# Prompt attention of a hybrid decoder step: probabilities turned unnormalised, product with V in query rows, one scaling per query tile, two score banks

## What is computed

```python
lo = jnp.einsum('bhqd,bhld->bhql', q, k_own) * HD_B ** -0.5
lo = jnp.where(own_pos[None, :] <= q_pos[:, None], lo, -jnp.inf)
p = jax.nn.softmax(concatenate([selected past block, lo]), axis=-1)
o = einsum(p, v)            # (512, 8, 64), all float32
```

## Time and profile before

| what | value |
|---|---|
| runs (3) | 1193.85, 1194.81, 1203.77 us; median 1194.81 |
| profiled execution | 1196.35 us, its span 1194.5 us |
| mean granted PE clock | 0.938 |
| busy | PE 1087.3 us (91%), DVE 648.0 (54%), ACT 468.7 (39%), POOL 256.4 (21%) |
| attention stage | 225.4 to 347.3 us of the span |

### The profile page before, as it was taken

The page is one execution under the profiler, slowest core; times in us unless marked ns, Lnnn a source line. Parts: engine busy times, 40 slices in busy tenths (PEclk is TensorE's granted clock), DMA queues, the critical chain, the costliest instruction groups (busy, mean ns, idle before and its releaser), DMA issues.

```text
span 1194.5 us, 21266 instructions
## 1 busy us (share of the span) xinstructions
PE 1087.3 (91%) x8054; PEld 1013.5 (85%) x8054; DVE 648.0 (54%) x892; ACT 468.7 (39%) x707; POOL 256.4 (21%) x113
## 2 busy tenths in 40 slices
PE   6999899698988589879968999999999999999997
PEld 6999799665677479668758799999999999999997
DVE  5228987897725774676544426555433433433443
ACT  6423554324333544554534122234413413523443
POOL 0035566776300353353330000000000000000000
PEclk8999899858998899989978899999999999999999
DMA  8376777655410245644547115433333332223311
GB/s 283 93 238 197 247 222 208 202 163 169 139 38 1 53 141 150 178 132 141 161 135 190 53 44 170 127 105 89 89 89 89 99 96 88 88 88 90 100 56 72
DMA packets 179256, 152.67 MB, mean 128 GB/s; under 512 B 8913, under 2 KB 141723, under 8 KB 178918
## 3 DMA queue, kind: packets, MB, share of 16 engines
q1 hardware_dynamic: 137414, 124.72, 35.5%
q10 hardware_dynamic: 41768, 26.91, 7.9%
HBM read 142.77 MB, written 8.93 MB: 127 GB/s over the span
## 4 chain that ended last, share of the span: by engine, by line
PE 76%; DVE 11%; ACT 5%; issue 4%; POOL 2%; ACTq 1%; DVEq 0%; POOLq 0%
PE ps L416 57%; PE ps L1795 6%; PE ps L1782 3%; DVE lg L1029 2%; POOL v_low L574 2%; PE ps L1682 1%; PE ps L1696 1%; DVE w_low L405 1%; PE ps L1539 1%; PE ps L1672 1%; ACTq L390 1%; DVE v_low L1261 1%; ACT v_high L827 1%; PE ps L1902 1%; ACT w_high L400 1%
## 5 line engine op out<-in xcount | busy, mean ns | idle before, releaser
L400 ACT ACTIVATE w_high<-w_raw 128x1024 fp32r<-128x1024 f32 x125 | 132.5, 1060 | 423.1 <-PE ps L416 399.8
L416 PE MATMUL ps<-xh,w_high 128*128 128x256 f32 x1216 | 257.5, 294 | 13.3 <-DVE w_low L405 7.4
L405 DVE TENSOR_TENSOR w_low<-w_raw,w_high 128x1024 fp32r<-128x1024 f32 x125 | 160.4, 1284 | 193.9 <-ACT w_high L400 193.6
L416 PE MATMUL ps<-xl,w_high 128*128 128x256 f32 x1216 | 250.0, 288 | 0.0
L416 PE MATMUL ps<-xh,w_low 128*128 128x256 f32 x1216 | 249.6, 287 | 0.0
L416 PEld LDWEIGHTS ps<-xh,w_high 128*128 128x128 f32 x1216 | 193.3, 194 | 21.1 <-issue 20.2
L416 PEld LDWEIGHTS ps<-xl,w_high 128*128 128x128 f32 x1216 | 193.7, 193 | 0.0
L416 PEld LDWEIGHTS ps<-xh,w_low 128*128 128x128 f32 x1216 | 193.6, 193 | 0.0
L557 POOL TENSOR_TENSOR ring<-ring,qb 128x1024 f32<-128x1024 f32 x64 | 158.5, 2488 | 158.7 <-DMA ring<-in_cache_k 87.0
L416 PE MATMUL ps<-mh,w_high 128*128 128x256 f32 (+1 forms) x640 | 129.3, 283 | 2.4 <-issue 2.4
L416 PE MATMUL ps<-mh,w_low 128*128 128x256 f32 (+1 forms) x640 | 129.5, 284 | 0.0
(11 more groups left out here) (358 smaller groups left out, 1498.0 us busy)
## 6 DMA issues: line engine op xcount, KB each, us to landing
ring<-in_cache_k SPq DMA_DIRECT2D x128, 256.0 KB, 3.0
ring<-in_cache_v SPq DMA_DIRECT2D x128, 256.0 KB, 2.9
w_raw<-in_w_in ACTq DMA_DIRECT2D x74, 256.0 KB, 4.0
w_raw<-in_w_up SPq DMA_DIRECT2D x64, 256.0 KB, 3.1
w_raw<-in_w_down SPq DMA_DIRECT2D x64, 256.0 KB, 2.9
w_raw<-in_w_in SPq DMA_DIRECT2D x16, 256.0 KB, 7.4
w_raw<-in_w_out SPq DMA_DIRECT2D x16, 256.0 KB, 3.0
ht_dram<-ht ACTq DMA_DIRECT2D x1, 2080.0 KB, 14.2
```

The costliest lines, as they stand in the source:

```text
L400: act.activation(w_high[:, u % 2], w_raw[:, s], ACT.Copy).then_inc(S_hi, 1)
L405: dve.tensor_tensor(w_low[:, u % 2], w_raw[:, u % 4], w_high[:, u % 2].bitcast(F32), ALU.subtract).then_inc(S_lo, 1)
L416: last = pe.matmul(out[:, a:b], w[:, u % 2, k, :], x[:, i, a:b], start=(first + i == 0 and w is w_high and x is rhs_h), stop=(first + i == ...
```

## The change

The probabilities are turned as they are, by a transpose with the identity. V is now the moving operand (64 columns) and the turned probabilities are the weights, so that the output has query rows and a head's 64 channels as columns, in bank 4 or 5 by query tile. When the eight heads of a query tile are done, DVE multiplies the 128 x 512 bank by the eight reciprocal sums per row into `att_n`, PE turns that back into the same bank with four transposes, and the two copies to `onb_h` and `onb_l` follow as before, from that bank. Scores have banks 0 and 1 only, so they are issued two ahead instead of three. The order within a query tile is set by heads 1 (scale), 2 (turn back), 3 (high part), 4 (low part) of the next one. The wait of the first V product of a tile for the low part is now for the tile two before.

```diff
-HIGH_AT, LOW_AT = 1, 3
+NORM_AT, TURN_AT, HIGH_AT, LOW_AT = 1, 2, 3, 4
...
+        att_n = at("att_n", [P, WB], F32, ht_at + 4 * NT * 4)
...
-        dg = at("dg", [P, 2, P], F32, pos[0])
...
         def score_bank(n, cols=512):
 
-            return bank((0, 1, 5)[n % 3], cols)
+            return bank(n % 2, cols)
+
+        def rows_bank(q_t):
+
+            return bank(4 + q_t % 2)
...
             def attention_high(c):
-                act.wait_ge(S["att_pv"], HB * (c + 1))
-                A(onb_h[:, :, c * P:(c + 1) * P], bank(4).rearrange("p (t c) -> p t c", t=4),
+                act.wait_ge(S["att_turned"], c + 1)
+                A(onb_h[:, :, c * P:(c + 1) * P], rows_bank(c).rearrange("p (t c) -> p t c", t=4),
...
-            def sums_inverse(n):
-
-                v.wait_ge(S["att_exp"], n + 1)
-                link(v.reciprocal(rrs[:, n % 2:n % 2 + 1], rs[:, n:n + 1]))
-                if n >= 2:
-                    v.wait_ge(S["pt_turned"], n - 1)
-                TS(dg[:, n % 2], ident, rrs[:, n % 2:n % 2 + 1], None, ALU.mult).then_inc(S["diag_out"], 1)
+            def normalise_rows(q_t):
+
+                v.wait_ge(S["att_exp"], HB * (q_t + 1))
+                if q_t:
+                    v.wait_ge(S["att_norm"], q_t)
+                link(v.reciprocal(rrs[:], rs[:, HB * q_t:HB * (q_t + 1)]))
+                if q_t:
+                    v.wait_ge(S["att_turned"], q_t)
+                v.wait_ge(S["att_pv"], HB * (q_t + 1))
+                TT(att_n[:].rearrange("p (h d) -> p h d", h=HB), rows_bank(q_t).rearrange("p (h d) -> p h d", h=HB),
+                   bc(rrs[:].rearrange("p (h o) -> p h o", o=1), [P, HB, DB]), ALU.mult).then_inc(S["att_norm"], 1)
...
-                if n >= 2:
-                    sums_inverse(n - 2)
...
+                if h == NORM_AT and q_t >= 1:
+                    normalise_rows(q_t - 1)
                 if h == LOW_AT and q_t >= 1:
                     attention_low(q_t - 1)
...
-            sums_inverse(NA - 2)
-            sums_inverse(NA - 1)
+            normalise_rows(3)
...
             def turn_probs(n):
 
-                pe.wait_ge(S["diag_out"], n + 1)
                 pe.wait_ge(S["att_exp"], n + 1)
                 if n >= 2:
                     pe.wait_ge(S["pt_out"], n - 1)
                 for t in range(n // HB + 1):
-                    last = mm(bank(2 + n % 2)[:, t * P:(t + 1) * P], prob[:, n % 2, t * P:(t + 1) * P], dg[:, n % 2],
-                              start=True, stop=True, skip_group_check=True)
+                    last = tr(bank(2 + n % 2)[:, t * P:(t + 1) * P], prob[:, n % 2, t * P:(t + 1) * P], ident)
...
-                if h == 0 and q_t >= 1:
-                    pe.wait_ge(S["onb_l_out"], q_t)
+                if h == 0 and q_t >= 2:
+                    pe.wait_ge(S["onb_l_out"], q_t - 1)
...
                 for t in range(q_t + 1):
-                    last = mm(bank(4)[rows, (h // 2) * P:(h // 2 + 1) * P], mtv[:, t, h * DB:(h + 1) * DB],
-                              probt[:, n % 2, t * P:(t + 1) * P], start=(t == 0), stop=(t == q_t),
-                              skip_group_check=True)
+                    last = mm(rows_bank(q_t)[:, h * DB:(h + 1) * DB], probt[:, n % 2, t * P:(t + 1) * P],
+                              mtv[:, t, h * DB:(h + 1) * DB], start=(t == 0), stop=(t == q_t), skip_group_check=True)
...
+            def turn_rows_out(q_t):
+
+                pe.wait_ge(S["att_norm"], q_t + 1)
+                turn4(4 + q_t % 2, [att_n[:, t * P:(t + 1) * P] for t in range(4)]).then_inc(S["att_turned"], 1)
...
-                if n + 3 < NA:
-                    scores(n + 3)
+                if n + 2 < NA:
+                    scores(n + 2)
                 if n >= 1:
                     pv_prompt(n - 1)
+                if n % HB == TURN_AT and n >= HB:
+                    turn_rows_out(n // HB - 1)
...
             pv_prompt(NA - 1)
+            turn_rows_out(3)
```

More of the change, by code:

```diff
@@ L339, in hybrid_step @@
             mh_out ml_out h_out sq2_out ssum_ready hx_h hx_l rel_out relsq_out uu_ready uh_out ul_out yt_turned
-            hw_out yf_sums yf_root yf_inv ys_out ys_done y_act y_dve v_scaled vb_masked vb_turned vb_out diag_out v_high_out v_low_pool v_low_dve""".split()
+            hw_out yf_sums yf_root yf_inv ys_out ys_done y_act y_dve v_scaled vb_masked vb_turned vb_out att_norm att_turned v_high_out v_low_pool v_low_dve""".split()
         S = {n: sem(n) for n in names}
@@ L1123, in attention_low @@
                 v.wait_ge(S["onb_h_out"], c + 1)
-                TT(onb_l[:, :, c * P:(c + 1) * P], bank(4).rearrange("p (t c) -> p t c", t=4),
+                TT(onb_l[:, :, c * P:(c + 1) * P], rows_bank(c).rearrange("p (t c) -> p t c", t=4),
                    onb_h[:, :, c * P:(c + 1) * P].bitcast(F32), ALU.subtract).then_inc(S["onb_l_out"], 1)
-            def sums_inverse(n):
-                v.wait_ge(S["att_exp"], n + 1)
-                link(v.reciprocal(rrs[:, n % 2:n % 2 + 1], rs[:, n:n + 1]))
-                if n >= 2:
-                    v.wait_ge(S["pt_turned"], n - 1)
-                TS(dg[:, n % 2], ident, rrs[:, n % 2:n % 2 + 1], None, ALU.mult).then_inc(S["diag_out"], 1)
+            def normalise_rows(q_t):
[8 more added lines that the diff above has]
+                   bc(rrs[:].rearrange("p (h o) -> p h o", o=1), [P, HB, DB]), ALU.mult).then_inc(S["att_norm"], 1)
             split_low(v, U_GATE + 2)
@@ L1667, in scores @@
                 r, N = slice(64 * (h % 2), 64 * (h % 2) + 64), (q_t + 1) * P
[L1668 to L1671, removed]
+                if n >= 2:
+                    pe.wait_ge(S["att_exp"], n - 1)
                 mm(score_bank(n, N), qt[r, h // 2, q_t * P:(q_t + 1) * P], kt[r, h // 2, 0:N], start=True, stop=True)\
@@ L1689, in pv_prompt @@
                 pe.wait_ge(S["pt_out"], n + 1)
-                if h == 0 and q_t >= 1:
-                    pe.wait_ge(S["onb_l_out"], q_t)
+                if h == 0 and q_t >= 2:
+                    pe.wait_ge(S["onb_l_out"], q_t - 1)
                 if n == 0:
                     pe.wait_ge(S["tm_out"], 12)
-                rows = slice(64 * (h % 2), 64 * (h % 2) + 64)
                 for t in range(q_t + 1):
-                    last = mm(bank(4)[rows, (h // 2) * P:(h // 2 + 1) * P], mtv[:, t, h * DB:(h + 1) * DB],
-                              probt[:, n % 2, t * P:(t + 1) * P], start=(t == 0), stop=(t == q_t),
-                              skip_group_check=True)
+                    last = mm(rows_bank(q_t)[:, h * DB:(h + 1) * DB], probt[:, n % 2, t * P:(t + 1) * P],
+                              mtv[:, t, h * DB:(h + 1) * DB], start=(t == 0), stop=(t == q_t), skip_group_check=True)
                 last.then_inc(S["att_pv"], 1)
+            def turn_rows_out(q_t):
+                pe.wait_ge(S["att_norm"], q_t + 1)
+                turn4(4 + q_t % 2, [att_n[:, t * P:(t + 1) * P] for t in range(4)]).then_inc(S["att_turned"], 1)
             scores(0)
             scores(1)
-            scores(2)
             gate_done = 0
```

## The result

| kernel | median of its runs | range | kernel before, same chip |
|---|---|---|---|
| changed, first comparison (4 runs) | 1189.18 us | 1173.94 to 1204.19 | 1194.33 |
| changed, second comparison (6 runs) | 1192.47 us | 1174.75 to 1200.85 | 1195.57 |

The ratio to the kernel before is 0.987 (95% interval 0.982 to 0.992) in the first comparison and 0.987 (0.981 to 0.993) in the second. It leaves out the longest runs, and here these are the ones in which the clock was low longest; with all runs counted the medians differ by 0.3 to 0.4% only. So the change is worth between nothing and 1.3%, and its own runs lie 30 us apart. My 1216 us lies above all ten of them, and I had forecast a slower kernel.

The account below looks back on a forecast made before the run. Prompt attention was taken as bound by DVE in its first half, PE in its second; with the clock low throughout, tile sums put it 19.7 us later, 21 with the tail: 1217.3 profiled, 1216 us median, range 1183 to 1223.

Parts of the forecast that it names:

- I expect no rise before the stage ends: Prompt attention: PE's clock stays at 1.2 GHz to the stage's end, since PE streams less per us between gates.
- rival B: Clock rises early in query tile 2 or 3, as V's weight-bound records keep PE's array busy: 1180 us, chance 0.18.
- C: Rival: the clock rises only about the start of query tile 4, so no change: 1195 us, chance 0.12.
- a stage end before 347 overturns it: Sign against the forecast: the prompt attention ending before 347 us, where about 368 was expected.
- the turns do count: Claim that transposes help raise PE's clock, read from spacing at the kernel's start falling from 0.21 to 0.11 us.
- The unit of 0.21 us for a transpose at 1.2 GHz: Turns on PE: one record of 128 columns a key tile, 0.21 us each at the lower clock, 0.11 at the higher.
- The term of 0.75 us an iteration for waits and first records: Attention iterations on PE at 1.2 GHz: about 0.75 us added to 5T units of 0.213 us in query tile T.
- Turning back: Four turns of four records on PE: 1.15 us each at 1.2 GHz; the last lets 1.2 us show in the tail.
- The gate share: Gate records between attention iterations on PE: six units each, half a share or 0.64 us per iteration at 1.2 GHz.
- The forecast case: Clock low throughout the prompt attention: stage 19.7 us later, 21 with the tail, 1216 us in all; chance 0.58.
- rival E: Loads, not DVE, pace query tile 1 at 3.4 us an iteration: 6 us added to any case; no separate chance.
- rival D: V's records take 0.107 us at 1.2 GHz, 15.3 us less than the forecast: 1201 us, chance 0.12.

Follow-up runs that it names:

- experiment 4: Changed kernel with its turns as float32 matmuls with the plain identity, two records a key tile instead of one: 1184.69 us, 0.990 of the kernel before.
- experiment 2: Changed kernel plus 144 matmuls of 256 columns that do no work on PE, before and between the turns: 1168.33 us, 0.977 of the kernel before.
- experiment 7: Kernel before with two score banks and scores issued two ahead, nothing else changed: 1256.76 us, 1.049 of the kernel before.
- experiment 6: Kernel before without scaled identity and normalisation, its turns made one-record transposes with the plain identity: 1199.14 us, 0.996 of the kernel before.
- experiment 5: Kernel before with turns by the plain identity, still matmuls; reciprocals, scaling and so normalisation left out: 1183.67 us, 0.988 of the kernel before.

## Why the prediction was wrong

*The step that failed* is "I expect no rise before the stage ends". In the profiled execution the clock rose at 298.7, in tile 3; in the second profile at 338.7; the mean clocks of the other eight runs lie from 0.913 to 0.939, on both sides of these. I had put 0.58 on one case out of something that comes out differently from run to run of the same program. The outcome lies between my rivals B (1180, a rise early in tile 2 or 3) and C (1195, about the start of tile 4). By my own test (a stage end before 347 overturns it) the first profile, with 333.9, overturns the forecast. The medians 1189 and 1192 us do lie in my range of 1183 to 1223, but only because it reached down to rivals to which I gave small chances; they lie on the other side of the kernel before than the 1216 I had forecast.

*The direction of the argument was right.* The changed kernel stays at 1.2 GHz longer than the one before: tile 2 at 0.50 instead of 0.90. With 80 records more on PE the first low stretch ended at 268.3 (experiment 4), not at 298.7 or 338.7, and with the filling there was none in the stage (experiment 2). Whether the number of records, the columns that they move or their kind counts is open.

*Two readings of the rows were wrong.* The digits of rows 1 are 8, 5, 8, 9, as said with the result. Rows 7 were read as transposes that bring the clock from 1.2 to 2.4 GHz, and on this rested "the turns do count", the disagreement with the Trainium skill, and the argument for rival B that turns alone raised the clock. The granted clock in both stretches of rows 7 is 1.00 (the number in front of the DMA share). Their spacing does fall from 0.21 to 0.11 us, but no rise of the clock is recorded there, so the trace neither contradicts the Trainium skill there nor bears it out. The unit of 0.21 us for a transpose at 1.2 GHz holds all the same: 0.85 us for four at 0.50 (258.85 to 259.70).

*Tile by tile*, predicted, first profile, second profile: start of the turns 230.5, 230.9, 230.0; tile 1 20.8, 19.1, 19.1; tile 2 29.3, 27.9, 27.9; tile 3 39.1, 30.4, 38.5; start of tile 4 to the tail 48, 25.6, 36.5. Even in the second profile the stage ends at 351.9, not 368. 9.3 us of that are the stretch at 1.00 behind 338.7, in which PE was busy throughout and which would have taken twice as long at 0.50. The rest are sizes:

*The term of 0.75 us an iteration for waits and first records* measured 0.46 and 0.48. In the second profile, at 1.2 GHz, PE:

```profile
319.74 1.06 PE L1686 MATMUL ps<-cf,prob 128*128 128x128 f32 x4
320.73 2.07 PE L1677 MATMUL ps<-kt,qt 64*128 64x512 f32 x2
322.73 1.97 PE L1698 MATMUL ps<-mtv,probt 128*128 128x64 f32 x8
324.46 0.78 PE L416 MATMUL ps<-xh,w_high 128*128 128x256 f32 x2
...
325.90 1.05 PE L1686 MATMUL ps<-cf,prob 128*128 128x128 f32 x4
```

From turn to gate 4.72 us, against 20 units of 0.213, 4.26: 0.46. In tile 2, from the rows above, 3.46 less 0.85 of turning back, less 2.13: 0.48. The iteration of before gave 0.63 (4.46 less 3.83), which I had rounded up. Over the 24 iterations of tiles 2 to 4 this is 7 us; tile 3 gives 0.9 of it back, as its last two iterations hold the longer scores of tile 4 (2.00 us for 1.57), which I had not counted. *Turning back* is 0.85 us each (258.85 to 259.70), not 1.15. *The gate share* is 1.44 us, so 0.72 per iteration, not 0.64. The forecast case, with the clock low to the end, would therefore have taken about 1210 us (stage end 351.9 + 9.3 = 361.2, 13.9 behind before), still above every run.

*Right:* the first turn waits for the exponential alone (230.9 for 230.5). DVE's work goes from 28.9 us to 3.6. Tile 1 took 2.4 us an iteration, with 2.6 forecast, but for another reason: PE, which I had called hidden, was busy 18.6 of 19.1 us. POOL took 2.41 us a product and waited 0.8 us for each load, 21.2 us in 28 products; rival E (3.4 us an iteration) falls. V's records are 0.22 us apart at 1.2 GHz (322.73 to 324.46 for eight), as long as a record that moves 128 columns, so half the columns saved no time there, and rival D falls. Two banks are not late in this change, though experiment 7 shows that this holds for the package alone. The turn of n = 17 comes 5.3 us behind the gate's end (277.88 to 283.21), for 5.2.

*The tail:* from the last turn to the tail's first transposes 6.6 us in the first profile, before 7.5 (339.77 to 347.28). So the turning back that I let show with 1.2 us does not show.

*What stays open:* what makes the clock rise at 298.7 in one run and at 338.7 in another of the same program. The runs here steer it only by adding or taking away records.

## What to carry to other kernels

Price an edit on a PE-bound stage in full-clock microseconds (span times mean granted clock), then ask separately whether the clock will follow; a change that takes records away between others can lower it and give the saving back, as some 20 us of full clock became 3 to 5 us between the medians here. Where the granted clock is 0.50 while PE is busy 10 of 10 us, a few full-width matmuls that do no work are worth a try; in the kernel before, where DVE set the pace of the first tile, they brought nothing. Before a difference between two kernels is put down to the stage that was edited, compare the stage's end in both profiles with the spans: in experiment 6 two thirds of the difference lay elsewhere. A wait that a change removes may be what made another of its parts free, so test the parts in both orders.

## What the runs showed of the hardware that I had not expected

- PE can be busy 87.8 of 89.7 us (249.0 to 338.7 in the second profile) and stay at 1.2 GHz, and the clock then rises among the same instructions.
- The same program has its rise at times 40 us apart: 1174 to 1204 us in ten runs, at 1096 to 1101 us of full clock. Six runs each of experiments 2, 4 and 5 spread over 9, 9 and 5 us.
- 144 matmuls of no use, 15.4 us of PE at 2.4 GHz (0.107 each), shorten a kernel of 1190 us by more than 20.
- With 80 records less on PE (experiment 5 to 6) the first low stretch of the stage lasts 54 us instead of 27, and the stage ends 5.8 us later.
